# A one-core decoder layer: weights in the order of use, and the last two expert pairs in halves

## What is computed

```python
g_sel = jnp.argmax(g_prob, axis=-1)                  # 1 of 4 groups
top_p, top_i = lax.top_k(e_prob, EXPERT_TOPK)        # 2 of its 8 experts
hg = jnp.einsum('td,edf->tef', ht, w_g)              # 32 experts, D=1024, f=256
hu = jnp.einsum('td,edf->tef', ht, w_u)
act = jax.nn.silu(hg) * hu * combine[..., None]
y = jnp.einsum('tef,efd->td', act, w_d)
x = x + gate_f * rmsnorm(y, g_post_ffn[l])           # the layer's output
```

## Time and profile before

| | us |
|---|---|
| median of 3 runs | 798.15 |
| lowest and highest run | 796.47, 798.77 |
| the profiled execution, whole | 795.45 |
| its span, first to last instruction | 793.6 |
| busy: PE, DVE, ACT, POOL | 702.3, 411.6, 287.9, 120.9 |

### The profile page before, as it was taken

The page is one execution under the profiler, slowest core; times in us unless marked ns, Lnnn a source line. Parts: engine busy times, 40 slices in busy tenths (PEclk is TensorE's granted clock), DMA queues, the critical chain, the costliest instruction groups (busy, mean ns, idle before and its releaser), DMA issues.

```text
span 793.6 us, 9709 instructions
## 1 busy us (share of the span) xinstructions
PE 702.3 (88%) x3447; PEld 445.4 (56%) x3447; DVE 411.6 (52%) x876; ACT 287.9 (36%) x512; POOL 120.9 (15%) x148
## 2 busy tenths in 40 slices
PE   1899989898999999999999799989889868788974
PEld 0447747566776777777777688763333323333321
DVE  2386958998897666644312735654351211112128
ACT  5133254254447778532232225342121211111224
POOL 3064852210002112000000001010122111111000
PEclk9999999999997999999999999999989998999998
DMA  9989730411311030303355162798999999999962
GB/s 343 388 302 369 285 136 1 115 57 50 107 46 61 2 106 2 107 0 107 107 212 185 60 234 79 293 407 322 416 417 420 419 422 419 419 419 421 403 272 106
DMA packets 49724, 179.27 MB, mean 226 GB/s; under 512 B 9560, under 2 KB 13762, under 8 KB 35340
## 3 DMA queue, kind: packets, MB, share of 16 engines
q1 hardware_dynamic: 43732, 166.26, 53.7%
q0 software_dynamic: 4784, 8.19, 2.9%
q10 hardware_dynamic: 1160, 4.20, 1.4%
HBM read 174.13 MB, written 12.59 MB: 235 GB/s over the span
## 4 chain that ended last, share of the span: by engine, by line
PE 53%; DVE 17%; DMA 8%; issue 7%; ACT 4%; DVEq 0%; POOL 0%; ACTq 0%; SPq 0%; POOLq 0%; PEldq 0%
PE psA L479 9%; PE psA L481 8%; PE psA L480 8%; PE psS L883 6%; PE psA L912 6%; PE psG L883 5%; DVE mk_mem L1833 3%; DVE m L1832 3%; DMA y_dram<-sig_mem,tables 2%; DMA arena<-y_dram 1%; PE psT L870 1%; DVE arena_r L1781 1%; DMA xn_dram<-sig_mem 1%; DMA arena<-in_w_out_dram 1%; DMA kv<-xn_dram,tables 1%
## 5 line engine op out<-in xcount | busy, mean ns | idle before, releaser
L479 PE MATMUL psA<-arena_r 128*128 128x512 f32 x320 | 130.1, 406 | 4.7 <-DVE arena_r L1781 4.1
L480 PE MATMUL psA<-arena_r 128*128 128x512 f32 x320 | 125.9, 393 | 0.0
L481 PE MATMUL psA<-arena_r 128*128 128x512 f32 x320 | 125.8, 393 | 0.0
L1781 DVE TENSOR_TENSOR arena_r<-arena,arena_r 128x1024 fp32r<-128x1024 f32 (+1 forms) x37 | 60.5, 1657 | 38.5 <-ACT arena_r L1305 37.6
L479 PEld LDWEIGHTS psA<-arena_r 128*128 128x128 f32 x320 | 60.9, 190 | 25.6 <-issue 13.7
L883 PE MATMUL psS<-arena,kv 128*64 128x512 f32 x224 | 64.6, 664 | 11.1 <-issue 10.9
L481 PEld LDWEIGHTS psA<-arena_r 128*128 128x128 f32 x320 | 60.7, 190 | 13.4
L480 PEld LDWEIGHTS psA<-arena_r 128*128 128x128 f32 x320 | 61.0, 191 | 12.0 <-issue 0.2
L883 PE MATMUL psG<-arena,kv 128*64 128x512 f32 x208 | 58.2, 611 | 4.8 <-issue 4.8
L1305 ACT CAST arena_r<-arena 128x1024 fp32r<-128x1024 f32 (+1 forms) x31 | 49.8, 1629 | 20.7 <-DMA arena<-in_w_in_dram 10.1
L2278 DVE TENSOR_TENSOR sig_mem<-sig_mem,psS 128x256 f32<-128x256 f32 x8 | 4.9, 613 | 81.7 <-ACT sig_mem L1624 81.7
(11 more groups left out here) (440 smaller groups left out, 1293.2 us busy)
## 6 DMA issues: line engine op xcount, KB each, us to landing
arena<-in_w_e_gate_dram SPq DMA_DIRECT2D x25, 1024.0 KB
arena<-in_w_e_up_dram SPq DMA_DIRECT2D x25, 1024.0 KB
arena<-in_w_in_dram SPq DMA_DIRECT2D x11, 2048.0 KB, 8.3
arena<-in_w_e_down_dram SPq DMA_DIRECT2D x12, 1024.0 KB, 15.6
qs_mem<-in_w_e_down_dram SPq DMA_DIRECT2D x10, 1024.0 KB, 19.7
arena<-in_w_ada_dram SPq DMA_DIRECT2D x4, 2048.0 KB, 17.1
qT<-in_w_ada_dram SPq DMA_DIRECT2D x6, 1024.0 KB, 5.4
gvs<-in_w_ada_dram SPq DMA_DIRECT2D x5, 1024.0 KB, 6.2
```

The costliest lines, as they stand in the source:

```text
L479: nc.tensor.matmul(acc, lhs[0], rhs[0], start=start, stop=False)
L480: nc.tensor.matmul(acc, lhs[0], rhs[1], start=False, stop=False)
L481: return nc.tensor.matmul(acc, lhs[1], rhs[0], start=False, stop=stop)
L1781: V.tensor_tensor(lo[:, part], src[:, part], hi[:, part], ALU.subtract).then_inc(lo_ready, 4 if q is None else 1)
```

## The change

SP's loads come in the order in which PE uses them: gate/up(j+1) before down(j). The gate/up loads of the last two pairs (14 and 15) are in halves, each with its own semaphore for the second half. OWN_DOWN is 14, so only pairs 14 and 15 have their down product behind their own gate/up product. The epilogue is written anew: nothing of it stands ahead of pair 15's last copies; the four tiles are combined one by one; only tile 0 is added by DVE, and tiles 1 to 3 are added on PE, now with the last_hot product first and the identity product behind it; ACT's dummy square root comes before the first scaled copies. The loads of y_dram are issued behind SP's branch for overflow pairs, in place of once before and once behind it. One small semaphore (ld_a2) is merged into ld_small.

```diff
@@ -54,7 +54,7 @@
 NPAIR = NE // 2
-OWN_DOWN = NPAIR - 3
+OWN_DOWN = NPAIR - 2
 NOV = 16
@@ -566,7 +567,7 @@
                     pe.wait_ge(gaT_ready, 1)
-                    pe.wait_ge(ld_a2, 16)
+                    pe.wait_ge(ld_small, 48)
                     z = take("G", ("z", r))
@@ -870,14 +871,14 @@
-            def gate_up_product(j, b, z, loads, g, g_turn, last_pair=False):
+            def gate_up_product(j, b, z, loads, g, g_turn, half_pair=None):
...
                     pe.wait_ge(h2g_ready[k // 4], 4 * j + k % 4 + 1)
-                    if last_pair and k == KD // 2:
-                        pe.wait_ge(we_last, 16 * 4)
+                    if half_pair is not None and k == KD // 2:
+                        pe.wait_ge(we_last[half_pair], 16 * 4)
                     for q, w in enumerate(gu_sets[z]):
@@ -914,7 +915,7 @@
             for j in range(NPAIR):
-                gate_up_product(j, j % 2, j % 3, j // 3, MOE_G[j % 2], j // 2, j == NPAIR - 1)
+                gate_up_product(j, j % 2, j % 3, j // 3, MOE_G[j % 2], j // 2, j - (NPAIR - 2) if j >= NPAIR - 2 else None)
                 if j == 0:
@@ -939,24 +940,34 @@
                     down_product(NPAIR + v, 0, 1, OV_LOADS + v)
-                pe.wait_ge(fss_ready, 4)
-            pe.wait_ge(yb_ready, NPAIR)
-            for tt in range(TT):
-                if tt >= 2:
-                    pe.wait_ge(sum_ready, (1, 3)[tt - 2])
+            def last_part(tt):
                 for half, (name, turns) in enumerate(sum_banks[tt]):
...
                     else:
-                        pe.wait_ge(bank[name].free, base[name] + turns)
-                    if tt >= 2:
-                        nc.tensor.matmul(ps[name][:, :], ident[:, :], yc[:, tt, 0, 512 * half:512 * (half + 1)], start=True, stop=False)
-                for half, (name, turns) in enumerate(sum_banks[tt]):
+                        pe.wait_ge(bank[name].free, base[name] + turns + (0 if name == "S0" else n_ov))
                     if half:
                         pe.wait_ge(yb_act, NPAIR)
-                    last = nc.tensor.matmul(ps[name][:, :], last_hot[:, tt, :], yb[:, 1, 512 * half:512 * (half + 1)], start=(tt < 2), stop=True)
+                    last = nc.tensor.matmul(ps[name][:, :], last_hot[:, tt, :], yb[:, 1, 512 * half:512 * (half + 1)], start=True, stop=(tt == 0))
+                if tt == 0:
+                    last.then_inc(sum_full, 1)
+            def other_part(tt):
+                pe.wait_ge(fss_ready, tt + 1)
+                for half, (name, _) in enumerate(sum_banks[tt]):
+                    last = nc.tensor.matmul(ps[name][:, :], ident[:, :], yc[:, tt, 0, 512 * half:512 * (half + 1)], start=False, stop=True)
                 last.then_inc(sum_full, 1)
+            pe.wait_ge(yb_ready, NPAIR)
+            for tt in range(3):
+                last_part(tt)
+            other_part(1)
+            last_part(3)
+            other_part(2)
+            other_part(3)
@@ -994,7 +1005,7 @@
             sp.dma_start(w_small[:, :, RANK:NS], win_v[:, :, O_IK:O_IK + 72]).then_inc(ld_small, 16)
-            sp.dma_start(a2[:, :], w_gla_a2[0]).then_inc(ld_a2, 16)
+            sp.dma_start(a2[:, :], w_gla_a2[0]).then_inc(ld_small, 16)
             def ada_load(m):
@@ -1028,18 +1039,23 @@
-            def experts(z, e0, e1_, g=None, g_turn=None, turn=None):
-                if g is not None:
-                    sp.wait_ge(bank[g].full, moe_base[g] + g_turn)
+            def next_gate_up(z, e0, e1_, g, g_turn):
+                sp.wait_ge(bank[g].full, moe_base[g] + g_turn)
                 gate_up(z, 0, e0)
                 gate_up(z, 1, e1_)
-                if turn is not None:
-                    sp.wait_ge(bank["A1"].full, moe_base["A1"] + turn)
+            def next_down(z, e0, e1_, turn):
+                sp.wait_ge(bank["A1"].full, moe_base["A1"] + turn)
                 down(z, 0, e0)
...
+            def pair_gate_up(j):
+                next_gate_up(j % 3, 2 * j, 2 * j + 1, MOE_G[(j - 3) % 2], (j - 3) // 2 + 1)
+            def pair_down(j):
+                next_down(j % 3, 2 * j, 2 * j + 1, j - 2)
@@ -1051,50 +1067,47 @@
             sp.wait_ge(ring_out, len(items))
+            gate_up(2, 0, 4)
+            gate_up(2, 1, 5)
             down(1, 0, 2)
             down(1, 1, 3)
-            gate_up(2, 0, 4)
-            gate_up(2, 1, 5)
             sp.wait_ge(x1_ready, 2 * TT)
...
             down(2, 1, 5)
-            for j in range(3, NPAIR - 1):
-                experts(j % 3, 2 * j, 2 * j + 1, MOE_G[(j - 3) % 2], (j - 3) // 2 + 1, j - 2)
-            j, z = NPAIR - 1, (NPAIR - 1) % 3
-            sp.wait_ge(bank[MOE_G[(j - 3) % 2]].full, moe_base[MOE_G[(j - 3) % 2]] + (j - 3) // 2 + 1)
-            for half in range(2):
-                part = slice(1024 * half, 1024 * (half + 1))
-                for q in range(2):
-                    for n, src in enumerate((weg_v, weu_v)):
-                        sp.dma_start(gu_sets[z][q][:, 2048 * n:2048 * (n + 1)][:, part], src[2 * j + q][:, part]).then_inc(we_last if half else we_in[z], 16)
-            sp.wait_ge(bank["A1"].full, moe_base["A1"] + j - 2)
-            for q in range(2):
-                down(z, q, 2 * j + q)
+            def pair_gate_up_halves(j):
+                z = j % 3
+                sp.wait_ge(bank[MOE_G[(j - 3) % 2]].full, moe_base[MOE_G[(j - 3) % 2]] + (j - 3) // 2 + 1)
+                for half in range(2):
+                    part = slice(1024 * half, 1024 * (half + 1))
+                    for q in range(2):
+                        for n, src in enumerate((weg_v, weu_v)):
+                            sp.dma_start(gu_sets[z][q][:, 2048 * n:2048 * (n + 1)][:, part], src[2 * j + q][:, part]).then_inc(we_last[j - (NPAIR - 2)] if half else we_in[z], 16)
+            pair_gate_up(3)
+            for j in range(3, NPAIR - 3):
+                pair_gate_up(j + 1)
+                pair_down(j)
+            pair_gate_up_halves(NPAIR - 2)
+            pair_down(NPAIR - 3)
+            pair_down(NPAIR - 2)
+            pair_gate_up_halves(NPAIR - 1)
+            pair_down(NPAIR - 1)
             y_v = y_dram.rearrange("(w t p) n -> t p w n", w=2, p=P)
-            def y_load():
-                for tt in range(TT):
-                    sp.dma_start(yc[:, tt, :, :], y_v[tt]).then_inc(yc_in[tt], 16)
-            for b in range(2):
-                sp.wait_ge(y_stored[b], 16 * (NPAIR // 2))
-            y_load()
             sp.wait_ge(slot_ready, 2)
...
             with sp.If(n_ov > 0):
-                sp.wait_ge(fss_ready, 2)
-                for tt in (2, 3):
-                    sp.wait_ge(yc_in[tt], 16)
                 with sp.Fori(0, n_ov) as v:
...
                     e_b = sp.value_load(ovi[0:1, bass.ds(2 * v + 1, 1)], min_val=0, max_val=NE - 1)
-                    experts(1, e_a, e_b, "G", NPAIR // 2 + v, NPAIR + v)
-                sp.wait_ge(y_stored[0], 16 * (NPAIR // 2 + n_ov))
-                y_load()
+                    next_gate_up(1, e_a, e_b, "G", NPAIR // 2 + v)
+                    next_down(1, e_a, e_b, NPAIR + v)
+            sp.wait_ge(y_stored[1], 16 * (NPAIR // 2))
+            sp.wait_ge(y_stored[0], 16 * (NPAIR // 2 + n_ov))
+            for tt in range(TT):
+                sp.dma_start(yc[:, tt, :, :], y_v[tt]).then_inc(yc_in[tt], 16)
             for tt in range(TT - 1):
@@ -1661,14 +1674,6 @@
                     act_taken(j, j % 2)
-            def first_choice(tt, loads, done):
-                act.wait_ge(yc_in[tt], 16 * loads)
-                nc.scalar.activation(yc[:, tt, 0, :], yc[:, tt, 0, :], ACT.Copy, scale=rt[:, 9, tt:tt + 1]).then_inc(done, 1)
-            first_choice(0, 1, fw_ready)
-            first_choice(1, 1, fw_ready)
             y_right(NPAIR - 1, 1, NPAIR // 2)
@@ -1676,26 +1681,39 @@
                     y_right(NPAIR + v, 0, NPAIR // 2 + v)
-                first_choice(0, 2, fw_ready)
-                first_choice(1, 2, fw_ready)
-                for tt in (2, 3):
-                    act.wait_ge(yc_in[tt], 32)
-            first_choice(2, 1, fw_late)
-            first_choice(3, 1, fw_late)
             scratch2 = stage_mem[:, 0:D]
-            nc.scalar.activation(st[:, 44:45], st[:, 34:35], ACT.Sqrt)
-            for tt in range(TT):
-                if tt < 2:
-                    act.wait_ge(sum_ready, (2, 4)[tt])
+            def first_choice(tt):
+                act.wait_ge(yc_in[tt], 16)
+                nc.scalar.activation(yc[:, tt, 0, :], yc[:, tt, 0, :], ACT.Copy, scale=rt[:, 9, tt:tt + 1]).then_inc(fw_ready, 1)
+            def square(tt):
+                if tt == 0:
+                    act.wait_ge(sum_ready, 1)
                     nc.scalar.activation(scratch2, yc[:, tt, 0, :], ACT.Square, accum_out=st[:, tt:tt + 1]).then_inc(fms_ready, 1)
-                else:
-                    act.wait_ge(sum_full, tt + 1)
-                    for half, (name, _) in enumerate(sum_banks[tt]):
-                        n = tt + 20 * half
```

(56 more changed lines are left out.)

9 lines of the change are left out of this document (5 added, 4 removed).

## The result

| | before | after |
|---|---|---|
| median of 20 runs, us | 797.51 | 791.57 |
| ratio to before, 95% interval | | 0.9932 [0.9918, 0.9947] |
| the profiled execution, its span | 795.45, 793.6 | 795.12, 793.4 |
| start of pair 0's gate/up product | 529.55 | 534.34 |
| **stage**: from there to the end of the span | 264.05 | 259.06 |

What follows compares the result with a forecast made beforehand. The weight stream bounds the expert stage. Pair 15's copy ends at 761.4, ACT's first scaled copy at 764.0, root 3 starts at 780.3, the end is 786.4: span -7.2 us, median 790.9, range 787.5 to 795.2.

Steps and rivals of the forecast that it cites:

- Part 1: Order of SP's weight loads: filling the hole before 555 us moves all later landings 3.3 us earlier (bounds 0 and 3.3).
- B: Weight stream: the hole is not saved, through a late down product 2 or gaps before 749; -3.9 us, chance 0.11.
- D: SP's queue runs dry at down(5), making the kernel slower; +3 us if down product 2 ends at 599; chance 0.05.
- Part 2: Last pairs on PE: earlier loads and halves start pair 15's down product at 757.1, a 5.1 us gain in PE's branch.
- The step that priced the halves of pair 14 at 0: SP's four extra load issues, at most 2.13 us each, are covered by early issue: 0, at worst 8.5 us.
- Rival C: Last loads: issue order is not landing order, so pair 15's last halves land at 756.7, not 751.6; -2.1 left, chance 0.07.
- A: Pair 14's store takes 13.5 us instead of 8.1, so the first y_dram tile comes at 767.0; -3.0 us, chance 0.12.
- Part 3: Epilogue: first scaled copy ends at 764.0 with the table load on the path, DVE takes 10.1 us, end at 786.4.
- the drain that the prediction cites: ACT's table load in the epilogue: a possible extra drain of about 1.38 us, cited but left out of the sum.
- Rival E: Reordering the loads does nothing and only the epilogue counts; -2.1 us, chance 0.03.

Runs made afterwards that it cites:

- hole_back: Changed kernel with one pair of loads back in the old order, down(3) ahead of gate/up(4); stage 262.30 us, ratio 0.9986 to before.
- whole_14: Changed kernel with pair 14's gate/up loads whole instead of in halves; stage 256.05 us, ratio 0.9884 to before.
- again: The changed kernel run and profiled once more, nothing altered; stage 257.48 us, ratio 0.9929 to before.
- epilogue_only: Changed kernel with the old load order, pair 14 whole and OWN_DOWN = NPAIR - 3; stage 262.05 us, ratio 0.9961 to before.
- order_only: Kernel before with the new load order, pair 14 in halves, OWN_DOWN = NPAIR - 2 and the merged semaphore; stage 257.96 us, ratio 0.9887 to before.
- order_whole: Kernel before with the new load order and pair 13's down product moved, pair 14 whole, pair 15 in halves; stage 260.11 us, ratio 0.9947 to before.
- table_early: Changed kernel with ACT's dummy square root moved ahead of its copy of pair 15's right half; stage 260.07 us, ratio 0.9926 to before.

## Why the prediction was right, and where it was off

The forecast was a stage of 256.85 (264.05 - 7.2); the two profiles of the changed kernel show 259.06 and 257.48, and the runs 5.4 us in place of 7.2. The mechanism and the sign were right, and some terms were mis-sized. That the predicted median of 790.9 is within 0.7 us of the measured 791.57 is partly luck: it starts from a median of three runs, 798.15, that lies 0.6 above the one of 20, and the medians lie further apart than the means.

**Part 1 was right in kind and size.** The hole is filled, its 3.3 us pass in full to the end (hole_back, 3.24), and pair 13 starts 9.0 earlier (8.3 forecast). Rivals B and D did not come: SP issues down(5) at s+54, and the share stays at 1.0.

**Part 2 reached nearly the forecast landing for a wrong reason.** Pair 15's last gate/up load lands at s+222.6 (forecast 751.6, s+222.05). The step that priced the halves of pair 14 at 0, on the ground that loads are issued 16 to 19 us ahead, failed: with them the last gate/up load lands 2 us later than in whole_14, though the stream moves its bytes at the same rate. In turn the landing gained more than the 3.3 of the hole: with pair 14 whole it moves by 4.8 (s+225.4 to s+220.6). By the packet records the last packet of all weights moves by only 3.7 (s+230.05 to s+226.35), near the hole; the other 1.1 us are that the gate/up load came in further ahead of the last down load. Rival C's premise, that order of issue is not order of landing, thus holds at this small scale, though its outcome didn't come. In after the second half of the product took 5.35 instead of 3.5, since the clock granted had fallen to half after the wait. That term, 1.8 us, was missing from the sum, though pair 13's product in the earlier trace rows has a stretch of the same kind (8.78 after a wait, against 7.09). In again it is absent, and down 15 is at s+228.5 against the forecast s+227.55.

**Rivals A and C.** y_dram was loaded at s+224.7, 1.5 earlier than forecast: pair 14's store was issued 1.6 earlier (750.8, s+216.5) and took 8.2 us where 8.1 were taken, so it was no limit. The prediction took the 5.8, 8.1 and 13.5 of the earlier trace rows for the stores alone. They are over the stores and the four loads; the stores before took 6.3 to 13.5 us, so its shortest store of 5.8 was a load. Pair 15's last gate/up load did not land with the last down load: no C.

**Part 3.** The first combine comes 7.46 after down 15 where 6.9 were worked out: ACT stands 0.59 us between its copy and the table load, around the branch that lies there, and this was not in the sum. DVE's chain to root 3 took 15.76 (16.3 forecast), the end after it 5.77 (6.14). No further table load appeared, and none of the drain that the prediction cites beside it: the first instruction behind the load at 769.30 starts at 770.59, as in the earlier trace rows. Together for after: 2.5 late at down 15, 0.6 late, 0.5 and 0.4 early, 2.2 in all: 256.85 + 2.2 = 259.05.

**Rival E**, the epilogue alone at -2.1, measured -2.0 in epilogue_only. What the prediction did not see is that the parts do not add: with the old epilogue the order alone is worth 6.1 us, because it brings the tiles of y_dram 6.2 us earlier. The new epilogue gives 2.0 under the old order, -1.1 under the new one with pair 14 in halves, and 4.1 with pair 14 whole (order_whole to whole_14).

The best two versions, whole_14 (0.9884) and order_only (0.9887), lie below the changed kernel (0.9932 and 0.9929), though their intervals overlap that of again.

## What to carry to other kernels

In a stage bound by its weight stream, look for the places where the queue runs empty: here an idle time of 3.3 us passed to the end at full price (3.24 us). PE's waits of 2 to 5 us ahead of the products in the middle are only the other side of that bound. At the tail of such a stage two branches race, here the last pair's product and the stores of the one before it, and an edit to the epilogue is worth what the branch it hangs on is late, so it has to be measured again when the loads are reordered. Splitting a load lets its first half be used earlier, but the product may then wait between the halves and go on at a lower clock, and here the last landing came later with more loads in halves, at an unchanged rate of the stream.

## What the runs showed of the hardware

With pair 14's four 1 MB loads split into eight of 512 KB, the last gate/up load of pair 15 landed 2 us later under one order of the loads (39.1 to 39.7 against 37.1 to 37.6 us over five and four kernels), while the bytes moved by s+216 were level within 0.3 MB (81.8 to 82.0 against 81.9 to 82.1); under the other order it did not (32.0 against 32.9). After a wait of 2.83 us the granted clock fell to 0.50 (1.2 GHz) within 1 us of the start of the next product (5.35 us for sixteen rows), and after one of 3.36 us it stayed at 1.00 (2.4 GHz, 3.65 us), in the same kernel at the same place. And a branch that is not entered had its effect on ACT: with a square root ahead of it and a silu in it, a table was loaded again behind it, 1.28 us (table_early), and passing it took 0.59 us between two instructions that otherwise follow each other without a gap.
